# Normalising the sparse branch's probabilities on GpSimd, head by head, in place of turned factors

## The reference

```python
h = rms_norm(x, g_mix[l]); proj = h @ w_in[l]
o_a = dsa_mixer(...)     # 8 heads of 64; each token attends to its 128 best-scored positions
o_b = nsa_mixer(...)     # 8 heads of 64: compressed + selected-block + window attention, gated
merged = sigmoid(gate_a_m) * (o_a @ w_up_a[l]) + sigmoid(gate_b_m) * (o_b @ w_up_b[l])
x = x + merged @ w_out[l]
x = x + square(relu(rms_norm(x, g_mlp[l]) @ w_ff1[l])) @ w_ff2[l]
```

```python
s = einsum('bthd,btkd->bthk', qb, ks) * HEAD_DIM ** -0.5 - slopes * dist
p = masked_softmax(s, dist >= 0)            # exp(s - max) / sum
return einsum('bthk,btkd->bthd', p, vs)
```

## Time and profile before

| what | value |
|---|---|
| median of 3 runs | 739.38 us (739.08 to 739.41) |
| the profiled execution | 739.83 us, its span 738.1 us |
| granted clock of TensorE | 0.999 |
| PE busy | 731.2 us of the span, 99% |
| DVE, ACT, POOL busy | 583.5, 437.4, 178.2 us |
| attention stage | about 100 to 331 us of the span |
| its DSA units | scores from 252.00 to 318.19 us |

### The profile page before, as it was taken

How to read it: one execution, slowest core, us unless ns; L and a number is a source line. 1 busy time by engine, 2 the same in 40 slices (tenths; PEclk the granted TensorE clock), 3 DMA queues, 4 the chain that set the end, 5 groups by cost and what they waited for, 6 DMA issues and landing times.

```text
span 738.1 us, 12691 instructions
## 1 busy us (share of the span) xinstructions
PE 731.2 (99%) x4686; PEld 651.5 (88%) x4686; DVE 583.5 (79%) x1079; ACT 437.4 (59%) x803; POOL 178.2 (24%) x192
## 2 busy tenths in 40 slices
PE   9999999999999999999999999999999999999998
PEld 9998987877997778777888899999999888799997
DVE  5478888779986877766667989888887788897987
ACT  7768487756677887654356555566556544533341
POOL 3110337424555544300012422222230000000000
PEclk9999999999999999999999999999999999999999
DMA  9621222102111121103533233333442333324342
GB/s 344 244 81 46 80 87 80 36 29 58 58 58 58 29 62 54 57 31 96 194 110 113 88 115 115 89 106 93 115 115 87 107 94 90 109 88 115 115 123 78
DMA packets 22861, 71.00 MB, mean 96 GB/s; under 512 B 2448, under 2 KB 5648, under 8 KB 22544
## 3 DMA queue, kind: packets, MB, share of 16 engines
q1 hardware_dynamic: 22656, 69.97, 30.5%
q10 hardware_dynamic: 144, 0.22, 0.1%
HBM read 68.08 MB, written 2.10 MB: 95 GB/s over the span
## 4 chain that ended last, share of the span: by engine, by line
PE 84%; DVE 8%; ACT 3%; issue 2%; DMA 1%; POOL 1%; DVEq 0%; SPq 0%; POOLq 0%
PE psum L2148 23%; PE psum L2150 23%; PE psum L2149 23%; PE psum L2156 5%; PE psum L2345 4%; PE psum L2322 2%; PE psum L2323 2%; DVE w_lo L1486 2%; DMA x2T<-in_xT 1%; ACT w_hi L1060 1%; POOL nrstd L958 1%; DVE cmp_in L1618 1%; DVE q_st L1642 1%; ACT h L1060 1%; DVE x2T L1853 1%
## 5 line engine op out<-in xcount | busy, mean ns | idle before, releaser
L1060 ACT ACTIVATE w_hi<-stage 128x512 fp32r<-128x512 f32 (+4 forms) x149 | 114.7, 778 | 32.0 <-PE psum L2150 26.8
L2148 PE MATMUL psum<-hT_hi,w_hi 128*128 128x256 f32 (+1 forms) x324 | 113.5, 350 | 0.3 <-DVE w_lo L1889 0.3
L2149 PE MATMUL psum<-hT_lo,w_hi 128*128 128x256 f32 (+1 forms) x324 | 107.3, 331 | 0.0
L2150 PE MATMUL psum<-hT_hi,w_lo 128*128 128x512 f32 (+1 forms) x264 | 90.6, 343 | 0.0
L1486 DVE TENSOR_TENSOR w_lo<-stage,w_hi 128x1024 fp32r<-128x1024 f32 (+4 forms) x58 | 56.7, 984 | 41.4 <-ACT w_hi L1060 37.2
L1060 ACT ACTIVATE w_hi<-s_sum 128x1024 fp32r<-128x1024 f32 x46 | 48.8, 1060 | 54.2 <-PE psum L2150 51.9
L2149 PE MATMUL psum<-a_lo,w_hi 128*128 128x512 f32 (+1 forms) x224 | 77.0, 344 | 0.0
L1248 ACT ACTIVATE prob<-prob,neg_max 128x128 f32<-128x128 f32 (+3 forms) x96 | 53.8, 560 | 32.1 <-DVE neg_max L1700 31.4
L1021 POOL TENSOR_TENSOR w_lo<-stage,w_hi 128x512 fp32r<-128x512 f32 x46 | 59.5, 1298 | 36.1 <-ACT w_hi L1060 36.1
L2149 PE MATMUL psum<-t_lo,w_hi 128*128 128x256 f32 x240 | 67.9, 283 | 0.0
L2148 PE MATMUL psum<-t_hi,w_hi 128*128 128x256 f32 x240 | 67.9, 283 | 0.0
(11 more groups left out here) (316 smaller groups left out, 2041.5 us busy)
## 6 DMA issues: line engine op xcount, KB each, us to landing
stage<-in_panels SPq DMA_DIRECT2D x104, 512.0 KB, 3.5
xT_in<-in_xT SPq DMA_DIRECT2D x8, 260.0 KB, 4.7
x_in<-in_x SPq DMA_DIRECT2D x4, 512.0 KB, 7.4
phi<-in_phi SPq DMA_DIRECT2D x2, 1024.0 KB, 6.3
x2T<-in_xT SPq DMA_DIRECT2D x1, 2048.0 KB, 9.0
stage<-in_panels SPq DMA_DIRECT2D x4, 408.0 KB, 3.2
stage<-in_panels SPq DMA_DIRECT2D x4, 384.0 KB, 4.3
stage<-in_panels SPq DMA_DIRECT2D x7, 212.0 KB, 4.9
```

Source lines behind the costliest of these rows:

```text
L1060: return nc.scalar.activation(dst, src, ACT.Copy, scale=scale)
L2148: mm(dst, a_h, b_h, start=start, stop=False)
L2149: mm(dst, a_h, b_l, start=False, stop=False)
L2150: return mm(dst, a_l, b_h, start=False, stop=stop)
```

## The change

In the DSA branch the probabilities are divided by their sum before they are turned. A new step `weigh` for unit u - 1 stands in step u, behind `qk` of unit u and ahead of `pT` of unit u - 3. In it DVE waits for the exponential of unit u - 1 and makes one inverse (128x1), and POOL waits for that and multiplies the unit's probabilities in place (128 x w). The transposes of a DSA unit wait for POOL where they waited for ACT. `inv`, `fac` and `close` are gone for the four DSA groups, and with them the tile `o_a`: `oT_hi` and `oT_low` read the output from its PSUM bank, and this bank is free when `oT_low` has read it, where `close` freed it. `OA_PLACES` changes from (85, 95, 96) to (85, 88, 93). SLC and WIN stay as they were, and PE's filler stays in its places.

```diff
-OB_PLACES, OA_PLACES = (70, 80, 81, 82), (85, 95, 96)
+OB_PLACES, OA_PLACES = (70, 80, 81, 82), (85, 88, 93)
...
+    WEIGHED = DSA
...
     for ti in range(NU // H):
-        at_unit(ti * H + 9, "inv", ti, at=early)
-        at_unit(ti * H + 10, "fac", ti)
+        if ti // TT < WEIGHED:
+            at_unit(ti * H + 9, "inv", ti, at=early)
+            at_unit(ti * H + 10, "fac", ti)
...
         if u < NU:
             step("qk", u)
+        if 1 <= u <= NU and units[u - 1][0] >= WEIGHED:
+            step("weigh", u - 1)
         if 0 <= u - T_LAG < NU:
             step("pT", u - T_LAG)
         if u < NU:
             step("exp", u)
-        if u >= TAKEN_AT and (u - TAKEN_AT) % H == 0:
+        if u >= TAKEN_AT and (u - TAKEN_AT) % H == 0 and (u - TAKEN_AT) // H < DSA * TT:
...
-    step("close", NU // H - 1)
...
-        def out_tile(m, tt):
-
-            return (o_b[:, tt, :, :], tt) if m else (o_a[:, tt % 2, :, :], TT + tt)
+        def out_tile(eng, m, tt):
+
+            if m:
+                return o_b[:, tt, :, :], tt
+            ps = wait_full(eng, ("O", DSA * TT + tt))
+            return ps.rearrange("p (k t) -> p k t", k=4), TT + tt
...
-            sp.wait_ge(oT_lo_done, 2 * TT)
+            for tt in (TT - 2, TT - 1):
+                wait_drained(sp, ("O", DSA * TT + tt))
...
+                elif kind == "weigh":
+                    u0, = a
+                    w = (units[u0][1] + 1) * P
+                    pool.wait_ge(unit_inv, u0 - WEIGHED * TT * H + 1)
+                    prob = probs[u0 % PROBS][:, 0:w]
+                    nc.gpsimd.tensor_tensor(prob, prob, row_inv[:, u0:u0 + 1].to_broadcast([P, w]), ALU.mult)\
+                        .then_inc(weighed, 1)
...
-                    src, n = out_tile(m, tt)
+                    src, n = out_tile(se, m, tt)
                     if m:
 
                         wait_full(se, ("O", 2 * TT - 1))
                         wait_drained(se, ("cmpO", tt))
+                        wait_drained(se, ("O", TT + tt))
                     else:
 
                         se.wait_ge(oT_lo_done, TT)
-                    wait_drained(se, ("O", TT * (1 if m else 2) + tt))
...
+                elif kind == "weigh":
+                    u, = a
+                    br, tt, h = units[u]
+                    ve.wait_ge(exp_done, u + 1)
+                    inv = row_inv[:, u:u + 1]
+                    if br == WIN:
+                        link(nc.vector.reciprocal(inv, row_sum[:, u:u + 1]))
+                        tt_op(inv, inv, gates[:, tt, h:h + 1, 1 + WIN], ALU.mult).then_inc(unit_inv, 1)
+                    else:
+                        nc.vector.reciprocal(inv, row_sum[:, u:u + 1]).then_inc(unit_inv, 1)
...
-                    wait_drained(ve, ("fac", ti))
+                    if br < WEIGHED:
+                        wait_drained(ve, ("fac", ti))
                     ps = wait_full(ve, ("O", ti)).rearrange("p (k t) -> p k t", k=4)
                     if br == WIN:
-                        link(tt_op(ps, ps, fac[:, :, :], ALU.mult))
+                        if br < WEIGHED:
+                            link(tt_op(ps, ps, fac[:, :, :], ALU.mult))
                         o = o_b[:, tt, :, :]
                         ins = tt_op(o, o, ps, ALU.add)
                     else:
-                        o = out_tile(br != DSA, tt)[0]
-                        if br == DSA and tt >= 2:
-                            ve.wait_ge(oT_lo_done, TT + tt - 1)
-                        ins = tt_op(o, ps, fac[:, :, :], ALU.mult)
+                        ins = tt_op(o_b[:, tt, :, :], ps, fac[:, :, :], ALU.mult)
                     drained(ins, ("O", ti))
                     wait_drained(ve, ("O", ti))
                 elif kind == "oT_low":
                     m, tt = a
-                    src, n = out_tile(m, tt)
+                    src, n = out_tile(ve, m, tt)
                     ve.wait_ge(oT_hi_done, n + 1)
                     tok = slice(tt * P, (tt + 1) * P)
-                    tt_op(oT_lo[m][:, :, tok], src, oT_hi[m][:, :, tok].bitcast(F32), ALU.subtract)\
-                        .then_inc(oT_lo_done, 1)
+                    ins = tt_op(oT_lo[m][:, :, tok], src, oT_hi[m][:, :, tok].bitcast(F32), ALU.subtract)
+                    if m:
+                        ins.then_inc(oT_lo_done, 1)
+                    else:
+                        drained(ins, ("O", DSA * TT + tt))
...
-                    te.wait_ge(exp_done, u + 1)
+                    if units[u][0] >= WEIGHED:
+                        te.wait_ge(weighed, u - WEIGHED * TT * H + 1)
+                    else:
+                        te.wait_ge(exp_done, u + 1)
...
-                        te.wait_ge(oT_lo_done, TT if m else 2 * TT)
+                        if m:
+                            te.wait_ge(oT_lo_done, TT)
+                        else:
+                            for tt in (TT - 2, TT - 1):
+                                wait_drained(te, ("O", DSA * TT + tt))
```

More of the change, by code:

```diff
@@ L551, in hybrid_layer @@
         relu = place("relu", [P, RELUS, S], Z + 59 * K)
-        o_a = place("o_a", [P, 2, 4, P], Z + 43 * K)
         cmp_e = place("cmp_e", [P, TT, H, CP], Z + 47 * K)
@@ L641, in hybrid_layer @@
         inv_done = sem("inv_done")
+        unit_inv = sem("unit_inv")
+        weighed = sem("weighed")
         fac_spread = sem("fac_spread")
```

## The result

The changed kernel takes 740.75 us in the median of 11 runs (739.61 to 743.09) against 739.41 us (739.08 to 740.22) for the kernel before, timed beside it: ratio 1.0021, 95% interval 1.0012 to 1.0031. So it is 1.34 us slower, where + 0.7 us was forecast. The forecast was 740.1 us, the range 737.5 to 742.3. The profiled execution took 740.67 us, with a span of 738.7 us; before it was 739.83 and 738.1.

What follows compares the result with a forecast made beforehand. PE, busy for 99% of the span, was taken to bound the kernel. Savings of 1.56 and 0.56 us against 2.8 us of new waits gave +0.7 on 739.38: 740.1 us, range 737.5 to 742.3 (forecast's own 739.2 to 741.1).

Steps and rivals of the forecast that it cites:

- The four groups of transposes: PE's four groups of `fac` transposes go: 2 x 0.43 + 2 x 0.35 = 1.56 us saved, all on the path.
- The gap: PE's gap behind the stage, 336.71 to 337.50, loses 0.56 us; the last close's removal saves that.
- The rival that it stays: The gap at 337.50 stays since the sigmoids keep PE waiting: 740.6 us, chance 0.06.
- Unit 67: Its multiplication waits behind gate tile g0_3 on POOL until 268.1; PE loses 0.7 us.
- walk: Unit-by-unit queueing of DVE's inverses and POOL's multiplications against the transposes' starts; new PE waits 2.8 us in sum.
- Unit 68: DVE, held for the previous unit's exponential, makes the row maximum 2.3 us later; PE loses 0.2 us.
- Unit 70: Two halves of panels and g0_4 stand in front of its multiplication on POOL; PE loses 0.5 us.
- Unit 76: POOL's queue, still late, reaches it at about 285.2, due at 285.0; PE loses 0.3 us.
- Unit 79: Its multiplication stands behind gate tile g0_6 on POOL, ready 287.85, due 287.18; PE loses 0.7 us.
- The third output's bank: Third DSA output reuses the first's bank, free only once `oT_low` has read it, at 302.4; PE loses 0.1 us.
- units 90 and 91: Last tile: a late inverse, then POOL's multiplications and a half panel; PE loses 0.3 us together.
- The slower rival: POOL bounds the last tile and the reused bank, 1.8 us more: 741.9 us, chance 0.27 (0.29 after the 0.2% band).

Runs made afterwards that it cites:

- e4: Kernel before, with the four DSA groups' factors spread by POOL but neither turned by PE nor copied by ACT; 738.89 us.
- e2: Changed kernel with POOL's gate tiles g0_3 to g0_7 moved behind its last multiplication; 738.79 us.
- e9: Changed kernel with the x2T reload issued two panels earlier, and DVE multiplying the probabilities in place of POOL; 741.04 us.
- e3: Changed kernel with DVE's inverse put later in its step, behind the copy of turned probabilities and other early steps; 741.29 us.
- e7: Changed kernel with gate tiles g0_3 to g0_7 behind POOL's last multiplication and ACT copying probT of units 87 and 95; 739.14 us.
- e8: e7 with the x2T reload also issued two panels earlier; 737.23 us.
- e10: Changed kernel with the x2T reload issued two panels earlier and the 32 inverses and multiplications left out; 737.15 us.
- e6: Kernel before, with the x2T reload issued two panels earlier; 738.82 us.
- e5: Changed kernel with the x2T reload issued two panels earlier; 739.46 us.
- e1: Changed kernel without the weighing: no inverse, no multiplication, DSA probabilities left undivided; 737.85 us.

## Why the prediction was right

The direction, the size and the mechanism came as forecast: PE's saving is smaller than its new waits for POOL. Step by step:

- **The four groups of transposes, 1.56 us.** They were worth 0.2 us more: by the start times 1.75 us in e4, and 0.41, 0.45, 0.45 and 0.46 in the changed kernel. A group behind other transposes was worth as much as one between products, since three transposes of `prob` take 0.32 us up to a group (309.41 to 309.73 in the kernel before) and 0.25 up to a matmul (308.78 to 309.03 in e4). What failed is the sentence that all of it is on the path: two groups covered DVE's copy of `probT`. In the changed kernel this came back as 0.35 and 0.30 us.
- **The gap, 0.56 us.** 0.79 became 0.38, so 0.41 us in the changed kernel. The rival that it stays did not hold. And there was not one gap but two: before, two matmuls of the same part start 0.41 and 0.34 us behind their predecessors (at 331.34 and 331.68), where 0.23 is the rule. These 0.28 us are gone in the changed kernel and still there in e4; what PE waited for I have not read.
- **Unit 67, 0.7 us.** 0.60, by the gate tile, as e2 and e9 show from two sides. The walk's own times, 268.5 less 267.93, give 0.57, and those of unit 68 give 0.1; both were entered 0.1 higher.
- **Unit 68, 0.2 us: nothing. Unit 70, 0.5 us: 0.77.** Unit 68's wait was hidden by unit 67's, and shows in e2 with 0.47. At unit 70 the late start of POOL's queue makes most of it (0.20 is left in e3), and g0_4, 0.45 us longer than in my walk, adds to it.
- **Unit 76, 0.3 us: 0.18. Unit 79, 0.7 us: 0.68**, behind g0_6, which started at 287.28.
- **The third output's bank, 0.1 us, and units 90 and 91, 0.3 us: nothing.** Here the walk set POOL and DVE against PE's old times and left out what PE had lost by then. PE came to the bank 1.6 us later than before (304.00 for 302.35), and DVE's subtraction had ended 0.17 us ahead of it (the row below); that the delay hid this wait I take for likely, but no run shows it. For unit 90 the multiplication ended at 315.48 and PE came at 315.64; in e7 and e8, where PE's earlier waits are gone, it waits 0.25 us. The slower rival needed both. DVE at the bank:

```profile
303.15 0.68 DVE L1838 TENSOR_TENSOR oT_lo<-psum,oT_hi 128x512 fp32r<-128x512 f32 x1
```

- **The sum.** Forecast 2.8 - 1.56 - 0.56 = + 0.7. Read in the profile: waits of 0.60 + 0.77 + 0.18 + 0.68 + 0.35 + 0.30 = 2.88, and twice 0.08 for the matmul behind a wait, less 1.77, 0.41 and 0.28: + 0.6; by the marks + 0.65. By e10 against e6 and e5 it splits into 1.91 us of saving and 2.49 us of cost from A to B. That this sum agrees so well with the forecast is in part luck: POOL's waits were forecast 0.6 us too high (2.8 for 2.2), the savings some 0.35 too low (2.12 for 2.46), and 0.65 us of waits for DVE were not in it, and these nearly cancel.
- **From the stage to the whole.** I took the median of the whole to follow the stage. It came out at + 1.34 us, nearly double the forecast, because the time from B to C depends on a reload that I had not priced; with the reload early the medians are 0.64 apart. That 740.75 us still lies in the forecast's own range (739.2 to 741.1) owes something to the width of that range. The upper bound of 5.5 us for the waits has no working: the slower rival's terms give 2.8 + 1.8 = 4.6. The reload was on the page: the chain that ended last named the DMA.

**The rule weighed** (the Trainium skill, SBUF — State Buffer, section "SBUF: two separate sides"). What it speaks of is seen again in the changed kernel: `oT_lo` 1.27 us from 273.06 on and g0_4 1.74 us from 273.74 on, where each is 0.68 and 1.30 alone. That section of the Trainium skill names besides DVE operations in a two-port performance mode. By that, the trace of e9 agrees, as far as it goes, for no row shows an operation's mode: the operation of one input at 299.94 took 1.41 us, and POOL scaled a gate tile from 299.78 to 301.07. In the changed kernel the same operation began ahead of the gate tile (300.27) and took 0.43:

```profile
299.96 0.43 DVE L1728 TENSOR_SCALAR score<-score 128x512 f32<-128x512 f32 x1
```

By this reading the collision cost the change up to 0.45 of the 0.77 us at unit 70, an estimate from the length of g0_4; no run took it away alone. I found no other such place where PE waits.

**Still open.** Why one and the same reload takes 8.3 us in one profile and 11.0 in another, and why the runs of the kernel before spread less (1.1 to 1.7 us) than those of the changed one and of e1, e2, e4 and e7 (3.5 to 4.9) and e3 (2.9), while without the reload's part all spread by 0.6 to 1.5. That DVE started at 369.0 in three of the profiles, whatever the time of issue, may be chance: in the others it was 367.5 to 370.7.

## What to carry to other kernels

An operation taken from the engine that sets the time is worth its length only where the next instruction would not have waited anyway: look for the copy that it covered. A small dependent step given to another engine is priced by the long operations that stand in front of it in that engine's in-order queue; moving five of them behind gained 1.76 us in the stage, and no cost showed elsewhere. Read the chain that ended last to its end, since a single large transfer behind the edited stage can double or hide a gain that is shown ahead of it.

## What was not expected of the hardware

POOL's multiplication by one broadcast value per row took 0.40, 0.63, 0.93 and 1.05 us in the mean for 128, 256, 384 and 512 columns; at the least 0.83 for 384 (302.85), on the line through the two forms of the earlier trace rows:

```profile
L1030 POOL TENSOR_TENSOR prob<-prob,row_inv 128x512 f32<-128x512 f32 x8 | 8.3, 1045 | 3.8 <-DVE row_inv L1812 3.8
L1030 POOL TENSOR_TENSOR prob<-prob,row_inv 128x384 f32<-128x384 f32 x8 | 7.4, 930 | 5.1 <-DVE row_inv L1812 5.1
L1030 POOL TENSOR_TENSOR prob<-prob,row_inv 128x256 f32<-128x256 f32 x8 | 4.9, 631 | 0.1
L1030 POOL TENSOR_TENSOR prob<-prob,row_inv 128x128 f32<-128x128 f32 x8 | 3.2, 401 | 5.4 <-DVE row_inv L1812 5.3
```

DVE's own in e9 took from 0.29 us to 1.22; for 512 columns 0.49 in seven of eight, 0.58 in the mean. An inverse of 128x1 takes 0.16 us, against 0.20 for the 128x8. One transfer of 2 MB took between 8.3 and 11.0 us from issue to landing, in seven kernels that load the same data in the same order. And a pause of 2.40 us on PE (e7, 411.87 to 414.27) went with a granted clock of 0.64 in the stretch of 413 to 416 us and 0.85 in the next, where one of 1.5 us at the same place (e1) left it at 1.00.
